# A decoder block with an expert layer: a later order of stores and loads, and the hits scaled four and four in the gates stage

## What is computed

```python
idx, gate = ...                      # 8 heads x 16 = 128 chosen experts per token, of 16384
u = jnp.take(expert_u, ib, axis=0)
a = jnp.einsum('tkd,td->tk', u, hb).astype(jnp.float32)
w = gb * jax.nn.gelu(a, approximate=False)
vsel = jnp.take(expert_v, ib, axis=0)
return jnp.einsum('tk,tkd->td', w.astype(vsel.dtype), vsel)
```

## Time and profile before

| | us |
|---|---|
| median of 3 runs | 1783.82 |
| lowest and highest | 1779.32, 1789.91 |
| the profiled execution: its time | 1788.98 |
| its span (first to last instruction) | 1787.2 |
| mean granted TensorE clock | 0.982 |

### The profile page before, as it was taken

One profiled execution on the slowest core, in us unless ns is written; L12 is line 12 of the kernel. 1 busy time (PEld: TensorE's weight loads), 2 busy tenths in 40 slices (PEclk: granted clock), 3 DMA queues, 4 the chain that ended last, 5 costly groups with the idle time before them and its releaser, 6 DMA issues. The chain is left out here.

```text
span 1787.2 us, 22493 instructions
## 1 busy us (share of the span) xinstructions
PE 1708.3 (96%) x7869; PEld 1411.2 (79%) x7869; DVE 1311.3 (73%) x2200; ACT 758.6 (42%) x1261; POOL 524.9 (29%) x423
## 2 busy tenths in 40 slices
PE   6999896989999999999998999999999999999997
PEld 5877675778877778888886888888788888888786
DVE  5787776559999969999994333333578868787878
ACT  5225344343322367777773222232333333333333
POOL 1000001115667610000000000000767668667750
PEclk9999998989999999999999999999999999999999
DMA  9563001332144435765667665553898999898985
GB/s 381 214 244 108 1 1 43 147 130 80 62 136 141 139 132 171 217 211 190 204 217 247 214 207 183 176 176 110 307 343 308 329 330 335 314 326 322 335 326 224
DMA packets 160415, 369.96 MB, mean 207 GB/s; under 512 B 16608, under 2 KB 78560, under 8 KB 157024
## 3 DMA queue, kind: packets, MB, share of 16 engines
q1 hardware_dynamic: 137824, 302.08, 48.5%
q0 software_dynamic: 22528, 67.19, 10.7%
HBM read 306.30 MB, written 62.91 MB: 207 GB/s over the span
## 5 line engine op out<-in xcount | busy, mean ns | idle before, releaser
L2022 PE MATMUL banks<-hl,actT 128*128 128x512 f32 x2268 | 518.3, 391 | 7.4 <-DVE actT L2244 7.3
L2022 PEld LDWEIGHTS banks<-hl,actT 128*128 128x128 f32 x2268 | 427.3, 189 | 98.1 <-DVE hl L2239 8.9
L1997 PE MATMUL banks<-actT,hl 128*128 128x512 f32 x1224 | 280.1, 391 | 7.0 <-ACT kept_acts L1931 6.7
L2154 POOL DMA_INDIRECT rows<-in_v,own_index x65 | 86.5, 1331 | 675.0 <-POOLq L1856 608.8
L1814 PE MATMUL banks<-actT,hl 128*128 128x512 f32 x1176 | 275.9, 390 | 1.8 <-PEq L1351 1.8
L1997 PEld LDWEIGHTS banks<-actT,hl 128*128 128x128 f32 x1224 | 231.2, 189 | 56.0 <-issue 7.8
L1814 PEld LDWEIGHTS banks<-actT,hl 128*128 128x128 f32 x1176 | 217.7, 188 | 45.3 <-issue 2.2
L2197 ACT ACTIVATE hl<-v_raw 128x1024 fp32r<-128x1024 f32 x125 | 132.4, 1059 | 273.3 <-PE banks L2022 206.9
L1592 PE MATMUL banks<-actT,hl 128*128 128x512 f32 x1032 | 241.5, 392 | 6.3 <-POOL hl L1439 5.0
L1592 PEld LDWEIGHTS banks<-actT,hl 128*128 128x128 f32 x1032 | 191.5, 188 | 49.6 <-POOL hl L1439 5.9
L2239 DVE TENSOR_TENSOR hl<-v_raw,hl 128x1024 fp32r<-128x1024 f32 x125 | 153.2, 1226 | 77.6 <-ACT hl L2197 57.2
(11 more groups left out here) (274 smaller groups left out, 2173.2 us busy)
## 6 DMA issues: line engine op xcount, KB each, us to landing
raw<-in_u SPq DMA_DIRECT2D x128, 512.0 KB, 3.9
v_raw<-in_v SPq DMA_DIRECT2D x128, 512.0 KB
expert_gates<-gates SPq DMA_DIRECT2D x12, 2048.0 KB, 9.8
group_gates<-expert_gates SPq DMA_DIRECT2D x32, 768.0 KB
wada<-in_w_ada SPq DMA_DIRECT2D x10, 2048.0 KB, 8.3
acts_in<-early_activations SPq DMA_DIRECT2D x100, 192.0 KB
early_activations<-kept_acts SPq DMA_DIRECT2D x52, 256.0 KB, 2.2
early_activations<-gate_acts SPq DMA_DIRECT2D x48, 256.0 KB, 2.3
```

What stands on the lines that cost most here:

```text
L1997: last = nc.tensor.matmul(m.psum[u % 2][:], hl[:, x, u % m.split, kc * P:(kc + 1) * P], m.actT[:, z, kc, :], start=(kc == 0 and j == 0), s ...
L2022: last = nc.tensor.matmul(bank(m, t, half)[:], w[:, x, t * P:(t + 1) * P], m.hl[:, z, j, half * S:(half + 1) * S], start=(first and k == 0 ...
L2154: nc.gpsimd.indirect_dma_start(out=fetched[k % FETCH], out_offset=None, in_=rows_of_v, in_offset=bass.IndirectOffsetOnAxis(ap=m.own_index[ ...
```

## The change

Seven edits:

- Gates stage: ScalarE scales four of eight tokens instead of three, VectorE four instead of five.
- Rest stage, SP's list: the loads of tiles 4 and 5 of u stand ahead of the waits on the stored gates and of the first two loads of gates. A store of a weighed tile stands two places later in the list (`LATE`).
- Rest stage, VectorE: the first weighing comes at iteration 5 instead of 3.
- Rest stage, SP's list: the activations of expert group 1 (`acts_in`) are loaded four tiles before the end instead of after the last store, and the gates of group 1 are loaded there as well, ahead of the last four stores; the experts stage no longer loads them. The gate buffers alternate from there on (`gate_buffer`).
- Own tokens: `own_rows` starts at tile 12 instead of 8 (128 rows over 116 tiles instead of 120).
- Own tokens: the fetches of activations run up to eight slots further ahead (`ahead`).
- Three semaphores instead of two count the landed chunks of activations.

```diff
-ACT_ROWS = 3
+ACT_ROWS = 4
...
+LATE = 8
...
-            for k in range(2):
-                sp.wait_ge(m.stored[k], 16 * GATE_PAIRS)
-            for u in range(RAW):
-                sp.wait_ge(acts_stored[u], 16 * stored_before)
-            load_gates(0)
-            load_gates(1)
-            for u in range(2):
-                sp.wait_ge(m.early_stored[u], 16 * EARLY // 2)
-            for n in range(RAW, count + RAW + 2):
+            for n in range(RAW, count + LATE):
+                if n == RAW + 2:
+                    for k in range(2):
+                        sp.wait_ge(m.stored[k], 16 * GATE_PAIRS)
+                    for u in range(RAW):
+                        sp.wait_ge(acts_stored[u], 16 * stored_before)
+                    load_gates(0)
+                    load_gates(1)
+                    for u in range(2):
+                        sp.wait_ge(m.early_stored[u], 16 * EARLY // 2)
...
-                if n >= RAW + 2:
-                    store(n - RAW - 2)
+                if n >= LATE:
+                    store(n - LATE)
...
-            for j in range(JG):
-                sp.dma_start(m.acts_in[:, j, :], a.early[TILES[JG + j], :, 0:SD]).then_inc(m.acts_landed[j], 16)
+                if n == count - JG:
+                    for j in range(JG):
+                        sp.dma_start(m.acts_in[:, j, :], a.early[TILES[JG + j], :, 0:SD]
+                                     ).then_inc(m.acts_landed[j], 16)
+                if n - LATE == count - JG - 1:
+                    free = (count // JG - 2) % 2
+                    sp.dma_start(gates[:, free].rearrange("p b j t -> p (b j t)"),
+                                 a.gates[:, SEQUENCE[1][0] * size:(SEQUENCE[1][0] + 1) * size]
+                                 ).then_inc(gates_landed[free], 16)
...
-                if n == 3:
-                    weigh(0)
-                    weigh(1)
-                if n >= 3:
+                if n == CLEAR:
+                    for k in range(CLEAR - 1):
+                        weigh(k)
+                if n >= CLEAR:
                     weigh(n - 1)
...
-        first_row = 8
+        first_row = 12
...
-                if s < GROUPS and kinds[s] == "plain":
+                if 2 <= s < GROUPS and kinds[s] == "plain":
                     load_gates(s)
...
-                    ).then_inc(act_landed[k // CHUNK_K % 2], 16)
+                    ).then_inc(act_landed[k // CHUNK_K % 3], 16)
...
+            def ahead(k):
+
+                return min(SLOTS, k + 1 + CHUNK_K + min(FETCH + 2, k // 2))
...
-                    if c < chunks - 1:
-                        fetch_act(k + CHUNK_K)
+                    for q in range(ahead(k - 1) if k else CHUNK_K, ahead(k)):
+                        fetch_act(q)
```

More of the change, by code:

```diff
@@ L2071, in stage_experts @@
         fetch_landed = [sem(f"fetch_landed{i}") for i in range(FETCH)]
-        act_landed = [sem("own_act_landed0"), sem("own_act_landed1")]
+        act_landed = [sem(f"own_act_landed{i}") for i in range(3)]
         fetch_read, own_weighed, own_added = sem("fetch_read"), sem("own_weighed"), sem("own_added")
@@ L2093, in loads_before, with gate_buffer @@
             return sum(k != "kept" for k in kinds[:n // JG])
+        def gate_buffer(q):
+            return (rest_groups + q) % 2
         def source(n):
@@ L2123, in load_gates @@
                 q = plain_before(s * JG) // JG
+                b = gate_buffer(q)
                 if q >= 2:
@@ L2126, in load_gates @@
                 at = SEQUENCE[s][0] * size
-                sp.dma_start(gates[:, q % 2].rearrange("p b j t -> p (b j t)"), a.gates[:, at:at + size]
-                             ).then_inc(gates_landed[q % 2], 16)
+                sp.dma_start(gates[:, b].rearrange("p b j t -> p (b j t)"), a.gates[:, at:at + size]
+                             ).then_inc(gates_landed[b], 16)
             for s in range(GROUPS + 1):
-                if s < GROUPS and kinds[s] == "plain":
+                if 2 <= s < GROUPS and kinds[s] == "plain":
                     load_gates(s)
@@ L2226, in weigh @@
                 q = i // JG
+                b = gate_buffer(q)
                 if j == 0:
-                    dve.wait_ge(gates_landed[q % 2], ((rest_groups + 1 - q % 2) // 2 + q // 2 + 1) * 16)
+                    dve.wait_ge(gates_landed[b], ((rest_groups + 1 - b) // 2 + q // 2 + 1) * 16)
                 dve.wait_ge(acts_landed[j], (loads_before(n) + 1) * 16)
@@ L2232, in weigh @@
                 V.tensor_tensor(weighed[:, i % 3, :].rearrange("p (b t) -> p b t", t=TB),
-                                acts[:, j, :].rearrange("p (b t) -> p b t", t=TB), gates[:, q % 2, :, j, :],
+                                acts[:, j, :].rearrange("p (b t) -> p b t", t=TB), gates[:, b, :, j, :],
                                 ALU.mult).then_inc(weighed_done, 1)
@@ L2247, in weigh_own @@
             def weigh_own(c):
-                dve.wait_ge(act_landed[c % 2], 16 * CHUNK_K * (c // 2 + 1))
+                dve.wait_ge(act_landed[c % 3], 16 * CHUNK_K * (c // 3 + 1))
                 ks = slice(c * CHUNK_K, (c + 1) * CHUNK_K)
```

## The result

The changed kernel took 1775.3 us in the median of 20 runs (1769.4 to 1789.9), the kernel before 1788.2 of 20 beside it (1779.3 to 1796.1): a ratio of 0.9938, with a 95% interval of 0.9922 to 0.9953. That is 12.9 us less between the medians, where 17.7 were forecast; the interval of the ratio stands for 8 to 14 us. The time lies just above the stated range, which ended at 1775. The profiled execution took 1778.76 us.

A forecast was written before the change was run, and what follows sets the result against it. TensorE, busy 96% of the span, was taken to bound the kernel, so only its gaps could be won: 5.7 + 2.15 + 3.2 + 2.6 + 4.1 = 17.7 us off 1783.8 gave 1766 us, range 1759 to 1775.

The forecast's parts named there:

- First seam: Between gates and rest stages: TensorE's 6.71 us wait shrinks to about 1.0, saving 5.7 us plus 2.15 for the clock.
- Second seam: Start of the experts stage: TensorE's 3.2 us wait for the low part of w goes, plus 2.6 us of clock.
- So all 3.2 us go, and the clock's share with them: Start of the experts stage: the whole wait vanishes, with 2.6 us for the clock; bounds 0 and 5.8 us.
- the 4.1 us of the later gaps: Experts stage, own tokens: VectorE's eight waits for activations go, and TensorE's three waits with them, 4.1 us.
- The 2.6 us for the clock: Experts stage start: 11.5 matmuls lost to the lower clock after the 3.18 us gap are won back, 2.6 us.
- Chunk 0 is issued as before but needed four tiles, 16 us, later: Experts stage, own tokens: the first chunk of activations keeps its issue time but is needed 16 us later.
- The stall that I named as what would make me wrong: Experts stage: the forecast is wrong if ScalarE waits for tiles of v long enough to stop TensorE.
- Four and four: Gates stage: four tokens each for ScalarE and VectorE; their loop 6.37 us against TensorE's 6.41, gain booked as zero.
- The rival that passes need over 0.473 us: Gates stage: ScalarE sets the pace; without overlap of its passes 35 us slower, 1801 us; chance 0.04.
- The first seam kept less than 1 us of its gap: Rival at gates to rest: the gap stays because tile issue blocks behind the store; 7.9 us not won, 1774; chance 0.09.
- Transfers did not pace the experts stage: Rival: the experts stage is limited by transfers at 321 GB/s, 7 us longer, 1773 us; chance 0.09.
- the gates stage did not get faster: Rival: VectorE paced TensorE in the gates stage after all, so 4 us more are won, 1762 us; chance 0.06.

The follow-up runs named there:

- v1: The kernel before, unchanged, profiled once more: a single execution of 1783.79 us.
- v2: The kernel before, unchanged, profiled for a third time: a single execution of 1785.8 us.
- y4: The kernel before with only the second seam's part (activations and gates of group 1 loaded early): 1788.26 us, ratio 1.0011.
- x3: The kernel before with only the first seam's part (tiles 4 and 5 of u early, later stores and first weighing): 1782.25 us, ratio 0.9976.
- y1: The changed kernel without the 128 gathers of activations, rows weighed with the gate squared: 1770.14 us, 0.9897 of the kernel before.
- w3: The changed kernel with ordinary transfers of 128 4-byte pieces in place of each gather: 1769.66 us, 0.9914 of the kernel before.
- y3: The changed kernel with the own rows from tile 8 again instead of 12: 1774.32 us, 0.9908 of the kernel before.

## Why the prediction was right in direction and 5 us too large

**The base.** The forecast of 1766 us stood on a median of three runs, 1783.8; the median of 20 is 1788.2. So of the 9.2 us between 1766.1 (1783.8 less 17.7) and 1775.3, 4.4 are the base, and 4.8 are a gain of 12.9 instead of 17.7. The profiled execution, 1788.98, which I took to be 5.2 us slow, was 0.8 above the median of 20. The rest of this section is about the 4.8.

**First seam: right, by its own steps.** TensorE is free at 969.27 here (969.73 less 0.46), 2.17 us later than before because the stages ahead ended later. Taken back by that, the high part starts at 965.87, where 966.1 to 966.9 stood; TensorE starts 1.69 us after it, as assumed. What I had wrong is SP: it does not issue the tiles at once but needs 6.41 us for the two, and is through at 964.5, a microsecond before the last packet of the store (965.5). The stretch became 292.8 - 283.6 = 9.2 us shorter (means of three and four executions). Forecast were 7.85. Of the rest, 0.5 is a wait before tile 1 of experts that became shorter and was not booked, and 0.9 the gap itself: 7.1 us became 0.5 in the means, where 6.7 and 1.0 were booked. In the trace of the changed kernel the first packet of tile 4 starts at 965.7, 0.2 us after the store's last. The rule of the Trainium skill, "DMA: Bandwidth & Descriptors", section "Queues, rings and completion order", that a queue row's descriptors are taken in ring order, agrees with that. The gap that it leaves was 0.3 to 0.9 us in the four executions.

**Second seam and own tokens: the mechanisms right, the sizes read from one execution.** All waits that were booked went, as forecast. But "So all 3.2 us go, and the clock's share with them" and the 4.1 us of the later gaps took one execution's rows for the kernel's. With the falls of the clock they were 11.4 us there, 5.5 in v1 and 5.7 in v2 (experts less 518.05), 7.5 in the mean. 9.9 were booked: **2.4 us too much**. The 2.6 us for the clock is the weakest part: two executions of three had no fall. For its own execution the sum was even too small, 9.9 for 11.4: the later waits add up to 4.1 in the list, and the starts of the matmuls stand 5.2 over their pace there.

**The step that failed** is "Chunk 0 is issued as before but needed four tiles, 16 us, later", and with it the second seam's "So all 3.2 us go": what the first burst of gathers does to the tiles of v beside it was put at nothing. The step looked only at who waits for these gathers, not at what they do to others. The stall that I named as what would make me wrong came, by that way or one beside it: ScalarE waited 7.8 us for the landing of tiles of v, though TensorE's first waits are for no tile. It cost 7.9, 0.3, 2.4 and 2.6 us in four executions, **3.3 in the mean**. In the kernel before, the tiles 9 to 11 are ordered up to 8 us later after the first gather (tile 10 at 9.2 to 13.2 us in its three executions, 5.4 in the changed kernel), and they were used in time. The gap at the second seam had hidden the collision: y4, which closes this gap alone, has the stall, and x3, which closes the first alone, has none.

All together: 17.7 + (9.2 - 7.85) - 2.4 - 3.3 = 13.4 us, against 12.9 between the medians, and inside the interval of 8 to 14. Without the stall it would be 16.7, and the two kernels without gathers have 17.0 (y1) and 15.2 us (w3) between the medians. That the gathers cause the stall rests on the profiles. It is there in seven of the eight that have the second seam closed and 16 gathers in one burst at the start of the stage, with TensorE's loop as it is, and in none of the two without gathers. The times alone do not show it clear of their scatter.

**Four and four: right.** The term is zero in both directions: 313.6 and 313.8 us with four, 313.8 with three. The round of ScalarE and VectorE was forecast at 6.37 us and is 6.36; VectorE's idle time before it adds is 0.24 ("up to some 0.4"), ScalarE's before its passes 0.52 (0.6). The loop's mean over the stage is 6.37. The rival that passes need over 0.473 us is out: 3.44 us for eight is 0.417 a step.

**The rivals.** The first seam kept less than 1 us of its gap, although the reason given for the rival came true: the issue of the two tiles is held behind the store, 6.41 us, and "SP issues them at once" was wrong. It was no loss because the tile had to wait for the store in any case. Transfers did not pace the experts stage (clean lengths of 518 us, 0.227 us a matmul), the gates stage did not get faster, ScalarE does not pace it. The fifth way, a collision of the gathers with the tiles of v, had no rival of its own; it should have had one.

**What stays open.** Why ScalarE takes up tiles of v late whose bytes are through, when gathers were issued just before, and why TensorE issues single matmuls then. The stall begins within a tile of TensorE's first jump back in its loop, and grows with the lateness of the tiles 9 to 11 of v (none up to 10.9 us; 1.2 at 14.9; 2.4 and 2.6 at 15.6; 4.7 to 8.2 at 18.7 to 19.5), but that order of things is seen, not shown: which of them is the cause of the other, or whether one thing holds up both engines, was not tried apart. Two things speak against the jump as the whole cause. In the changed kernel and in y3 the first wait stands before the last matmuls of tile 7, ahead of the jump; and a load of TensorE's instructions at the jump is not seen: between 1244 and 1308 us the trace of the changed kernel has no packet of the two instruction queues (q8 and q14 on the page). Many records of landings are missing from 1250 to 1281, so lateness is read from ScalarE's starts.

## What to carry to other kernels

A gap that is closed moves its engine earlier into everything behind it: ask which burst it now meets, and price that as its own rival. Terms read from gaps of one execution scatter by half their size, those with a fall of the clock above all; where the kernel can be profiled more than once, take the mean. Many small gathers in a row are not free for the engines that wait for other transfers beside them, even where nobody waits for the gathers; look for them when an engine takes up a tile late. Shorter bursts took the stall away at one place and left a smaller one at another. And when a tile seems late, compare its last packet with its first use before blaming the transfer. A base of three runs was 4.4 us off here, nearly as much as the sum.

## What the runs showed of the hardware

- With GpSimd's gathers of 128 pieces of 4 bytes, 16 in some 20 us, the latest of three tiles of 512 KB in SP's queue was used 10.4 to 19.5 us after its issue in the changed kernel's four executions, instead of 9.1. In the one with 19.5 its bytes were through 14.1 us before that. 17 ordinary transfers of 128 such pieces in 9.1 us did nothing of the kind.
- TensorE stood with "issue" waits of 0.3 to 1.5 us, mostly one matmul between two of them, at such a time.
- A gap of 3.45 us left the clock at 2.4 GHz (v1), one of 3.18 us was followed by 1.2 GHz. In these rows the length of the gap alone does not decide.
- SP's issue of two loads behind a store in the same queue took 6.41 and 7.49 us, where one load alone takes 0.44 (1252.85).
